# A two-layer trunk of attention, convolution and expert retrieval: roots of the norms by token columns, the first two tiles of a norm together, empty attention keys left out, C from U tile 40, the x update beside the last V tile, and a new order of the first loads

## The reference

```python
mod = silu(c) @ ada_w[l] + ada_b[l]
sh1, sc1, g1, sh2, sc2, g2 = split(mod, 6)
h = rms_norm(x, norm_mix_g[l]) * (1 + sc1) + sh1
x = x + g1 * hybrid_mixer(h, ...)
h = rms_norm(x, norm_ffn_g[l]) * (1 + sc2) + sh2
x = x + g2 * peer(h, ...)

# hybrid_mixer
q, k, v, glu, gates = split(h @ w_in)
q, k = rope(rms_norm(q)), rope(rms_norm(k))
attn = windowed_attention(q, k, v, sinks) @ w_o_attn   # 16 heads, 4 kv heads, window 128, blocks of 128
u = ga * sigmoid(gb)                                    # glu = ga, gb
u = silu(layer_norm(causal_depthwise_conv(u)))          # 31 taps
conv = u @ w_o_conv
return (sigmoid(g_attn) * attn + sigmoid(g_conv) * conv) @ w_out

# peer: 8 heads, 128 x 128 experts
s = scores of (h @ w_query) against two sets of 128 sub-keys; top 16 of each, then the top 16 of their sums
y = sum over heads and their 16 experts of softmax(top) * gelu(u_tab[e] . h) * v_tab[e]
```

## Time and profile before

| | us |
|---|---|
| median of 3 runs (lowest, highest) | 3812.41 (3807.12, 3818.23) |
| the profiled execution | 3803.47 |
| its span | 3801.6 |
| TensorE matmul busy | 3587.4 (94%) |
| VectorE busy | 3123.0 (82%) |
| ScalarE busy | 1588.9 (42%) |
| GpSimd busy | 1337.8 (35%) |
| share of TensorE's clock granted, mean | 0.981 |
| DMA, mean | 227 GB/s |

### The profile page before, as it was taken

One profiled execution on the slowest core, in us unless ns is written; L12 is line 12 of the kernel. 1 busy time (PEld: TensorE's weight loads), 2 busy tenths in 40 slices (PEclk: granted clock), 3 DMA queues, 4 the chain that ended last, 5 costly groups with the idle time before them and its releaser, 6 DMA issues.

```text
span 3801.6 us, 61085 instructions
## 1 busy us (share of the span) xinstructions
PE 3587.4 (94%) x19138; PEld 3253.7 (86%) x19138; DVE 3123.0 (82%) x6277; ACT 1588.9 (42%) x2323; POOL 1337.8 (35%) x1132
## 2 busy tenths in 40 slices
PE   4999999988999999999979998999899999999998
PEld 2766676988999999999957666779899999999998
DVE  6799876997888878888857997679988888788887
ACT  3366234433545433333344644244344544333332
POOL 0000002463555545454300000035445555455544
PEclk9999999999999999999999999999899999999999
DMA  4111263455999899999911112724479998999997
GB/s 174 66 49 55 74 223 110 134 176 196 324 342 339 280 343 350 344 351 345 319 65 56 50 61 74 258 89 155 135 259 340 342 321 289 347 345 341 351 346 256
DMA packets 407297, 862.52 MB, mean 227 GB/s; under 512 B 165376, under 2 KB 230912, under 8 KB 406528
## 3 DMA queue, kind: packets, MB, share of 16 engines
q1 hardware_dynamic: 296160, 538.70, 42.1%
q0 software_dynamic: 73728, 268.47, 20.1%
q10 hardware_dynamic: 37152, 52.45, 3.7%
HBM read 773.49 MB, written 85.98 MB: 226 GB/s over the span
## 4 chain that ended last, share of the span: by engine, by line
PE 60%; DVE 23%; issue 8%; ACT 4%; DMA 4%; SPq 0%; DVEq 0%; ACTq 0%
PE ps L538 9%; PE ps L763 9%; PE ps L762 9%; PE ps L540 9%; PE ps L764 9%; PE ps L539 9%; PE ps L736 3%; DMA raw<-stream 3%; DVE yT L1225 2%; DVE oneR L1561 2%; DVE i L1434 2%; DVE eq L1498 2%; DVE eq L1505 2%; DVE gbuf L1422 1%; DVE v L1430 1%
## 5 line engine op out<-in xcount | busy, mean ns | idle before, releaser
L538 PE MATMUL ps<-h_hi,w_hi 128*128 128x384 f32 (+1 forms) x3008 | 1100.9, 366 | 80.2 <-DVE h_lo L1150 36.0
L801 ACT CAST w_hi<-raw 128x1024 fp32r<-128x1024 f32 x680 | 715.1, 1054 | 900.2 <-DMA raw<-stream 857.0
L540 PE MATMUL ps<-h_hi,w_lo 128*128 128x384 f32 (+1 forms) x3008 | 1069.2, 355 | 0.0
L539 PE MATMUL ps<-h_lo,w_hi 128*128 128x384 f32 (+1 forms) x3008 | 1068.2, 355 | 0.0
L538 PEld LDWEIGHTS ps<-h_hi,w_hi 128*128 128x128 f32 x3008 | 572.4, 190 | 151.1 <-DVE h_lo L1150 35.6
L762 PE MATMUL ps<-cf_hi,w_hi 128*128 128x384 f32 x2048 | 688.8, 336 | 10.0 <-DVE cf_lo L1592 5.0
L763 PE MATMUL ps<-cf_lo,w_hi 128*128 128x384 f32 x2048 | 690.4, 337 | 0.0
L764 PE MATMUL ps<-cf_hi,w_lo 128*128 128x384 f32 x2048 | 688.8, 336 | 0.0
L514 POOL TENSOR_TENSOR spare<-spare 128x1 f32<-128x1 f32 x504 | 327.4, 650 | 944.5 <-DVE y_sp L1577 480.5
L539 PEld LDWEIGHTS ps<-h_lo,w_hi 128*128 128x128 f32 x3008 | 573.0, 190 | 41.3 <-issue 6.9
L540 PEld LDWEIGHTS ps<-h_hi,w_lo 128*128 128x128 f32 x3008 | 571.1, 190 | 40.7
(11 more groups left out here) (224 smaller groups left out, 4885.4 us busy)
## 6 DMA issues: line engine op xcount, KB each, us to landing
raw<-stream SPq DMA_DIRECT2D x680, 512.0 KB
gelu_scratch<-g_out ACTq DMA_DIRECT2D x256, 192.0 KB, 5.4
cg<-gelu_scratch SPq DMA_DIRECT2D x256, 192.0 KB, 6.2
c_scratch<-stage SPq DMA_DIRECT2D x64, 512.0 KB, 8.5
cg<-c_scratch SPq DMA_DIRECT2D x256, 128.0 KB, 5.2
qT<-ada SPq DMA_DIRECT2D x32, 512.0 KB, 5.8
cgate<-ada SPq DMA_DIRECT2D x32, 512.0 KB, 5.5
w_rows<-ada SPq DMA_DIRECT2D x32, 512.0 KB, 7.0
```

Source lines behind the costliest of these rows:

```text
L538: nc.tensor.matmul(ps[:, b, 0:n], wh, hi[:, c, t0:T], start=c == 0, stop=False)
L539: nc.tensor.matmul(ps[:, b, 0:n], wh, lo[:, c, t0:T], start=False, stop=False)
L540: mm = nc.tensor.matmul(ps[:, b, 0:n], wl, hi[:, c, t0:T], start=False, stop=c == C - 1)
L801: nc.scalar.copy(w_hi[:, s], raw[:, s]).then_inc(hi_done, 1)
```

## The change

- **Launch**: x and the 16 rows are issued by ScalarE, ahead of its Silu; SyncE issues positions, constants, c and parameters and goes straight on to the first four weight tiles. The parameters and the scale `gs` are prepared by functions that stand ahead of the loop and at the end of a layer.
- **Roots by token columns**: the matmuls of a norm's sums are turned round (squares stationary, 2 columns of a matrix of 1/D moving), so that token sums come as 8 columns. ScalarE takes their root, VectorE the reciprocal, then builds four diagonal matrices of 128 tokens; TensorE multiplies each with the matrix of 1/D, which spreads the inverse root over all rows of a PSUM bank, from which `hx` is made. The table of the root is loaded ahead of the squares.
- **First pair**: the first two tiles of each of the three norms of a layer take each chunk together.
- **Keys**: second banks for the sums of squares and the rotation. The scale of the second half of the queries is made before `masked(1)`.
- **Empty keys**: units of the first block work on 128 keys; the memsets of `kT` and `vn` go.
- **Tiles**: `U_ROUTE` 36, `EXP_TILES` (6, 14, 23, 32), the sparse gather from U tile 18, C from tile 40 over 78 tiles.
- **End of a layer**: the last V tile goes chunk by chunk in order, each with its transpose; VectorE updates x and ScalarE squares behind it. The output goes out in eight loads of 256 KB.

The diff, cut to its core:

```diff
-U_ROUTE = 32
-C_FIRST, C_TILES = 36, 82
+U_ROUTE = 36
+C_FIRST, C_TILES = 40, 78
-EXP_TILES = (6, 14, 22, 29)
+EXP_TILES = (6, 14, 23, 32)
+GATHER_TILE = 18
+def own(n):
+    return P if n == 0 else 0
...
 # SyncE
-            sp.dma_start(con[:], con_d).then_inc(const_in, 16)
+            sp.dma_start(pos_i[:], pos_d.broadcast_to([P, T])).then_inc(rope_in, 16)
+            sp.dma_start(con[:], con_d).then_inc(rope_in, 16)
+            sp.dma_start(cact[:], c_d.broadcast_to([P, D])).then_inc(c_in, 16)
             sp.dma_start(params[:], params_d).then_inc(const_in, 16)
-            for n in range(ADA_1):
-                sp.dma_start(rows0[:, n], ada[n]).then_inc(ada_in[n // 4], 16)
-                if n == 7:
-                    sp.dma_start(xT[:], x_d).then_inc(x_in, 16)
...
-            sp.wait_ge(x_upd, DEPTH * C)
-            sp.dma_start(out_d, xT[:]).then_inc(out_st, 16)
+            for c in range(C):
+                sp.wait_ge(x_upd, DEPTH * C + c + 1)
+                sp.dma_start(out_d[:, c], xT[:, c]).then_inc(out_st, 16)
...
 # TensorE
+                def first_pair(i, hi, lo, chunks):
+                    for q in range(2):
+                        pe.wait_ge(bank_read[q], l * (NE // 2) + i // 2 + 1)
+                    pe.wait_ge(lo_done, l * NT + i + 6)
+                    for c in range(C):
+                        pe.wait_ge(chunks[0], chunks[1] + c + 1)
+                        for q in range(2):
+                            wh, wl = w_hi[:, (i + q) % 4, c], w_lo[:, (i + q) % 4, c]
+                            nc.tensor.matmul(ps[:, q], wh, hi[:, c], start=c == 0, stop=False)
+                            nc.tensor.matmul(ps[:, q], wh, lo[:, c], start=False, stop=False)
+                            mm = nc.tensor.matmul(ps[:, q], wl, hi[:, c], start=False, stop=c == C - 1)
+                            if c == C - 1:
+                                mm.then_inc(tile_done, 1)
+                def token_sums(b, c):
+                    for tt in range(NB):
+                        mm = nc.tensor.matmul(ps[:, b, 2 * tt:2 * tt + 2], sq[:, c % 2, tt * P:(tt + 1) * P],
+                                              mean[:, 0:2], start=c + tt == 0, stop=c == C - 1 and tt == NB - 1)
+                    return mm
+                def spread(b, k):
+                    for tt in range(NB):
+                        pe.wait_ge(diag_done, NB * k + tt + 1)
+                        mm = nc.tensor.matmul(ps[:, b, tt * P:(tt + 1) * P], mean, rstd[:, tt * P:(tt + 1) * P],
+                                              start=True, stop=True)
+                    mm.then_inc(rs_wide, 1)
...
-                for i in range(I_Q + C):
-                    proj(i, h_hi, h_lo, (h_ready, 2 * l * C) if i == 0 else None)
+                first_pair(0, h_hi, h_lo, (h_ready, 2 * l * C))
+                for i in range(2, I_Q + C):
+                    proj(i, h_hi, h_lo)
...
                 for c in range(C):
                     pe.wait_ge(ln_sq, l * C + c + 1)
-                    nc.tensor.matmul(ps[:, 6], ones, sq[:, c % 2], start=c == 0, stop=c == C - 1).then_inc(ln_mm, 1)
+                    token_sums(6, c).then_inc(ln_mm, 1)
+                spread(5, 3 * l + 1)
                 for i in range(I_CG + 3, I_CG + FIRST_GATES):
                     proj(i, h_hi, h_lo)
-                for m in range(FIRST_GATES):
-                    proj(I_CG + FIRST_GATES + m, n_hi, n_lo, (ln_lo, l * C) if m == 0 else None)
+                first_pair(I_CG + FIRST_GATES, n_hi, n_lo, (ln_lo, l * C))
+                for m in range(2, FIRST_GATES):
+                    proj(I_CG + FIRST_GATES + m, n_hi, n_lo)
...
 # TensorE, experts()
-                    for c in W_ORDER:
+                    for c in range(C) if last else W_ORDER:
...
+                        if last:
+                            if c == C - 1:
+                                mm.then_inc(tile_done, 1)
+                            if c == 0:
+                                pe.wait_ge(row_used, (l + 1) * 2 * P + 4)
+                            nc.tensor.transpose(ps[:, c, 0:P], y_sp[:, c * P:(c + 1) * P], ident).then_inc(y_tr, 1)
...
 # ScalarE
+            act.dma_start(xT[:], x_d).then_inc(x_in, 16)
+            for n in range(ADA_1):
+                act.dma_start(rows0[:, n], ada[n]).then_inc(ada_in[n // 4], 16)
+            act.wait_ge(c_in, 16)
             nc.scalar.activation(cact[:], cact[:], ACT.Silu).then_inc(c_silu, 1)
...
+                def root_table():
+                    nc.scalar.activation(spare[:, 30:31], eps, ACT.Sqrt)
+                def token_root(b):
+                    nc.scalar.activation(rs[:], ps[:, b, 0:2 * NB], ACT.Sqrt, scale=1.0 / D ** 2,
+                                         bias=eps).then_inc(rt_done, 1)
                 def norm(w):
+                    root_table()
...
                 high_at(I_CG + 4)
                 first_gate(2)
+                root_table()
                 for c in range(2, C):
                     centred_square(c)
                 high_at(I_CG + 5)
                 act.wait_ge(ln_mm, l * 2 * C + 2 * C)
-                nc.scalar.activation(rstd[:], ps[:, 6], ACT.Sqrt, scale=1.0 / D, bias=eps).then_inc(ln_silu, 1)
+                token_root(6)
...
                     nc.scalar.copy(n_hi[:, c], hs[:, c % 2]).then_inc(ln_hi, 1)
                 first_gate(3)
...
 # VectorE
+                def inverse_roots(k):
+                    dve.wait_ge(rt_done, k + 1)
+                    nc.vector.reciprocal(rs[:], rs[:]).then_inc(rs_done, 1)
+                    dve.wait_ge(rs_done, k + 1)
+                    for tt in range(NB):
+                        nc.vector.tensor_scalar(rstd[:, tt * P:(tt + 1) * P], ident, rs[:, 2 * tt:2 * tt + 1], None,
+                                                ALU.mult).then_inc(diag_done, 1)
...
+                parameters(slice(1, 2))
+                prepare(l + 1)
                 for c in range(C):
+                    dve.wait_ge(y_tr, l * C + c + 1)
```

More of the change, by code:

```diff
@@ L54 @@
 ADA_2 = 6 * C
-LN_STEPS = 2 * C + 2
+LN_STEPS = 2 * C
 PAIRS = ((0, 3, TOPK), (3, TOPK, 4))
@@ L554, in norm_sums @@
                         pe.wait_ge(sq_done, (2 * l + w) * C + c + 1)
-                        nc.tensor.matmul(ps[:, 7], ones, sq[:, c % 2], start=c == 0,
-                                         stop=c == C - 1).then_inc(sq_used, 1)
+                        token_sums(7 * w, c).then_inc(sq_used, 1)
+                    spread(7 - w, 3 * l + 2 * w)
                 norm_sums(0)
@@ L608, in turned @@
                         pe.wait_ge(p_ev, l * 2 * UNITS + 2 * u)
-                    for kb in range(2):
+                    if u == 0:
+                        pe.wait_ge(qa, l * 10 + 9)
+                        pe.wait_ge(rq_done, l * 2 + 2)
+                    alone = unit(u)[0] == 0
+                    for kb in range(int(alone), 2):
                         for r in range(R):
@@ L620, in values @@
                         pe.wait_ge(o_lod, l * UNITS + u)
-                    for kb in range(2):
+                    for kb in range(int(n == 0), 2):
                         pe.wait_ge(p_ev, l * 2 * UNITS + 2 * u + kb + 1)
@@ L666, in channel_sum @@
                     pe.wait_ge(conv_step, l * C * TAPS + (c // 2 + 1) * 2 * TAPS)
-                    nc.tensor.matmul(ps[:, 7], ones, yT[:, c], start=c == 0, stop=c == C - 1).then_inc(ln_mm, 1)
+                    nc.tensor.matmul(ps[:, 7], mean, yT[:, c], start=c == 0, stop=c == C - 1).then_inc(ln_mm, 1)
                 pe.wait_ge(o_lod, l * UNITS + UNITS)
@@ L704, in half_scores @@
                     mm.then_inc(r_mm, 1)
[L706 to L709 removed]
+                first_pair(I_QRY, h_hi, h_lo, (h_ready, 2 * l * C + C))
+                half_scores(0)
+                for i in range(I_QRY + 2, I_U):
+                    proj(i, h_hi, h_lo)
+                    half_scores(i - 1 - I_QRY)
                 half_scores(I_U - 1 - I_QRY)
```

171 lines of the change are left out of this document (82 added, 89 removed).

## The result

The changed kernel takes **3781.2 us** (median of 4 runs, 3779.4 to 3787.1) against 3814.6 us (4 runs, 3807.1 to 3818.2): the ratio is 0.9909, interval 0.9894 to 0.9924, a gain of 33 us. The forecast was 3735 with a range of 3710 to 3766. The sign was right; the time lies 15 us above the range.

The account below looks back on a forecast made before the run. TensorE was taken as the bound, busy 3587 of 3802 us. Launch 4.8 + 3.6, layers twice 21.4, between layers 13.0 and end 7.0 sum to 71.2 us: 3732.3, adjusted for run differences to 3735 us, range 3710 to 3766.

Parts of the forecast that it names:

- The sums are no cheaper: a token sum is 8 small matmuls at 0.11 us spacing: In the norms: token sums cost 0.9 us a chunk against 0.86 for the feature sums.
- the root chain: Second norm, behind the sums: root, reciprocal, diagonals and spread by token columns bring `hx` 2.2 us earlier (1 to 3).
- The convolution: Tiles 48 and 49 wait for the gate of tile 47 despite `hx` 1.7 us earlier: 5.6 us lost a layer.
- The pair at the other norms: First two tiles together at the mixer and PEER norms: 3.6 and 3.8 us gained (2 to 5).
- Launch: Start of the kernel: loads on ScalarE, free at 18 us, bring `hx` at 53 instead of 57.8, 4.8 us gained.
- the rival that had 0.10: Launch: ScalarE is held longer, nothing gained and two or three us lost, 3742 us; chance 0.10.
- as forecast (12.3): Routing, U tiles: four more tiles routed, less VectorE's delay by GpSimd's subtractions, gain 12.3 us a layer.
- TensorE would wait 8 us there: U tile 36: VectorE's end of routing still decides, with a wait of some 8 us for its `w_lo`.
- The 3 forecast for the one-hots: C over 78 tiles: denser groups make TensorE wait more for one-hots, 3 us a layer lost (0 to 12).
- Keys, attention, boundary and end: Gains: keys 5.2 and empty keys in attention 6.5 us a layer, between layers 13.0 with the pair, end 7.0.
- The rival of the clock falling in C: Stage C: single-tile groups wait 2.4 us and run at 1.2 GHz after, up to 3883 us; chance 0.04.
- That of the port: Routing: each of four more GpSimd subtractions blocks VectorE fully, 8.6 us instead of 4.3, 3744 us; chance 0.12.

Follow-up runs that it names:

- e8: Changed kernel with 128 moving columns in the token sums, convolution tiles 48 and 49 one after the other, 960 unused bytes behind the constants: 3730.1 us, ratio 0.9775.
- e13: e9 with the 17 launch loads of x and the rows issued by SyncE: 3720.4 us, ratio 0.9759 to the kernel before.
- e5: Changed kernel with 960 unused bytes a partition behind the constants, no instruction changed: 3765.7 us, ratio 0.986 to the kernel before.
- e12: Changed kernel with the first two tiles behind the mixer and PEER norms one after the other, the convolution's pair kept: 3789.9 us, ratio 0.9944.
- e10: Changed kernel with the 17 loads of x and the modulation rows issued by SyncE instead of ScalarE: 3785.0 us, ratio 0.9913.
- e9: e8 with 128 unused bytes in the place of 960, moving operands whole multiples of 512 bytes behind `h_hi`: 3729.5 us, ratio 0.9768.
- e1: Changed kernel with sums, root and reciprocal over 512 columns again in all three norms: 3781.1 us, ratio 0.9923.

## Why the prediction was wrong

Three causes, taken away together in e8, give 51 us back. Of these 11 are a loss in the convolution that the prediction had counted, so the three explain 40 of the 46 us between forecast and result. Without that loss the forecast would be 3724 us, and e8 takes 3730; that the two are so near owes something to luck, since smaller terms were off both ways.

*The token sums.* "The sums are no cheaper: a token sum is 8 small matmuls at 0.11 us spacing" is the step that failed. The spacing came from feature sums that stand between tiles; in a row of 64 such matmuls the clock falls to 1.2 GHz while TensorE is busy, the spacing is 0.21, and the sums are 3.5 us longer in the second norm and 5.3 in the convolution. Of the 2.2 us forecast for the root chain behind them 1.2 came: from the sums' end to `hx` are 3.0 us, and 4.2 before, since the spread takes 2.08 us at the low clock. In e13, where it takes 1.16, they are 2.1. Having taken the clock from idle stretches alone, the prediction did not ask what fills the engine.

*The convolution.* The mechanism was right and so was the place: idle of 8 to 9 us between tiles 47 and 48, ended by the gate. Only the size was off, -12.1 and -11.2 for -5.6: `hx`, forecast 1.7 us earlier, came some 4 us later relative to the stage's start (459.58, with the stage 14.4 us ahead, against 470.06), from the first cause. Leaving the pair out gives 7.7 us back in layer 0.

*The places of the tensors.* The prediction has no term for it. The change shows it only as a constant (NCON from 1155 to 900) and one new small tensor; it moved every tensor behind them by 960 bytes and cost 15 us (e5). No row of before could price it.

*The pair at the other norms* was forecast at 14.8 us for four and is worth 8.7 (e12). By its own terms (6.3 less 2.4 less 0.6) the forecast should have been 3.3 us each, 13.2. That its first matmuls run at the half clock (0.80 us for the first one at 604.88) is the likely reason; it was not tested alone.

*Launch.* 4.8 forecast, 1.7 had. ScalarE was held until 22.6 and not 18, the condition of the rival that had 0.10, which went further and had nothing gained; when that was undone the sums took its place, as e10 and e13 show together. By the Trainium skill, DMA: Bandwidth & Descriptors, Issuing engines are not separate DMA queues, the move to another engine brings no earlier landing, since all share the same 16 DMA engines. The traces agree: what is loaded at launch is in by 38.7 us when ScalarE issues the rows beside the first weights, with a row as the last, and by 38.4 when SyncE issues all of it in a row (e10), with a weight tile as the last; the last row then lands at 33.4.

*U, C and W.* U tile 36 starts 19.0 us earlier; of that 2.2 are the stages before, and about 5 stood ahead of this tile in the kernel before alone: 3.4 for the transposes behind the routing and the wait after them, which the changed kernel has behind tile 36, and 1.5 at 1.2 GHz in tile 32. That leaves 12 us, as forecast (12.3). That TensorE would wait 8 us there was wrong; the gathers, put at tile 18, took 5.9 of it earlier, at no cost. C then gave back some 6 us and not 3. The 3 forecast for the one-hots came: idle from 900 us on to W is 12.2 us against 9.1, and their waits grew by 5.6 us for both layers. The rest is mainly the clock, which the prediction left out here: 6.8 us at 1.2 GHz follow tile 36, where in the kernel before such a stretch (867 to 874 us) lay ahead of it.

*Keys, attention, boundary and end* were right within 1.5 us each (the 125.1 us given for the start of tile 9 is 124.6 in the trace). The rival of the clock falling in C did not happen: from 895 us to the end of the stage it is 1.00. That of the port did not either: counted from the stage's start, TensorE gets its first `w_lo` from VectorE 4.9 us later than before (873.74 with the stage 2.2 us ahead, against 871.03), near the 4.3 of the sum and not the 8.6 of the rival.

## What to carry to other kernels

Price a run of small matmuls by a row in which they stand in a row, clock beside it, and not by their spacing between large ones; widening the moving operand was free here and worth 18 us. When a change alters the size of any resident tensor, compare the matmul spacing of a stage that it doesn't touch: 2 ns in 174, over the 256 tiles of W, are 13 us, as large as most edits. And a new wait for two buffers at once takes the later of two evacuations, so look at who reads the second one and what stands ahead of that read.

## What the runs showed of the hardware

A matmul's time depends on where its moving operand (the one whose columns are counted) begins, at a whole clock with nothing waiting. Worked out from the starts of successive matmuls (24 to a tile), with the place in a partition in bytes behind `h_hi`, modulo 512:

```
operands (512 columns)       modulo 512    ns per matmul    traces
h_hi, h_lo                      0            226.7           all
o_hi, o_lo                      0            226.7           e9
o_hi, o_lo                    320            228.9           before, e5, e8
o_hi, o_lo                    384            233.5           after
W, four slots (384 columns)
cf_hi 320, cf_lo 320 or 0                    173.2 to 174.2  before, e5, e8
cf_hi 384, cf_lo 384 or 0                    175.4 to 176.1  after, e1
cf_hi 0, cf_lo 0                             173.3 to 173.4  e9
```

The figures are those of matmuls in full flow; after a stop up to ten at the start of a tile take 224 to 236 ns each, and the very first over 300, in the traces of before and after alike. The pattern within a tile is the same in 27 of 28 tiles of a slot (for slots 0 and 1 of W after: 174.2, 175.0, 181.6, 175.8, 173.4 ns, and again; slot 3 repeats three values).

The expectation of e9 calls the quick places multiples of 512 bytes. That holds only when counted from `h_hi`. In the program that the kernel files build, `h_hi` begins at byte 32896 of a partition, 128 past a multiple of 512; `o_hi` begins 128 past one in e9, 448 past in the kernel before and in e5, and in the changed kernel, the slowest of the three, exactly on one (134656). The stationary operands `w_hi` and `w_lo` lie ahead of the constants, also 128 past a multiple, and did not move. Whether the place itself counts or its distance from the weights, no run separates; no other places were tried, and why they differ is open.

In the launch the windows show a clock of 1.00 over the token sums, though 58 matmuls in 12 us are as slow as at 1.2 GHz elsewhere. That 1.00 is not a reading: the trace of the changed kernel has no record of the clock before 65.2 us (that of the kernel before none before 48.0), and a window without a record prints 1.00.
